# Sums of squares in a two-block transformer kernel: head sums in four column groups, and squares added on GpSimd ahead of two matmuls

## The reference

```
def rms_norm(x, gain):
    y = x * rsqrt(mean(x * x, axis=-1) + EPS)
    return y * gain

# first block
h = h + mixer(rms_norm(h, norm_mix))      # 1st normalisation; w_in, two attentions, w_out
#   inside: fox heads: rms_norm(fq heads, fox_q_gain), rms_norm(fk heads, fox_k_gain)
h = h + peer(rms_norm(h, norm_ffn))       # 2nd; w_query, top-k of keys, peer_u, peer_v
# second block
h = modulate(rms_norm(h, norm1_g), ...)   # 3rd; w_in_2: attention (q, k normalised by head), S5 scan, gates
h = modulate(rms_norm(h, norm2_g), ...)   # 4th; w_up, convolution, w_down
```

## Time and profile before

| | |
|---|---|
| median of 3 runs | 3751.93 us (3750.91 to 3752.04) |
| time of the profiled execution | 3747.92 us |
| its span, first to last instruction | 3746.3 us |
| TensorE matmul busy | 3612.7 us, 96% |
| VectorE busy | 2572.4 us, 69% |
| ScalarE busy | 2113.1 us, 56% |
| GpSimd busy | 71.1 us, 2% |
| mean granted TensorE clock | 0.987 |

### The profile page before, as it was taken

The page is one execution under the profiler, slowest core; times in us unless marked ns, Lnnn a source line. Parts: engine busy times, 40 slices in busy tenths (PEclk is TensorE's granted clock), DMA queues, the critical chain, the costliest instruction groups (busy, mean ns, idle before and its releaser), DMA issues.

```text
span 3746.3 us, 75816 instructions
## 1 busy us (share of the span) xinstructions
PE 3612.7 (96%) x26600; PEld 3390.2 (90%) x26600; DVE 2572.4 (69%) x4815; ACT 2113.1 (56%) x3811; POOL 71.1 (2%) x137
## 2 busy tenths in 40 slices
PE   7999998999999999999999989999988899999998
PEld 6999998999999999787888879889988899999998
DVE  5775647788877777555688868887656666666555
ACT  4446644666667776454555555554554566666453
POOL 1000000000000000000000000000000000000000
PEclk9999999999999999999999999999999999999999
DMA  7854457555554444566788844444444455555554
GB/s 262 313 195 148 149 197 286 187 178 178 176 178 161 159 162 152 173 212 213 269 330 331 328 157 139 154 132 143 148 154 157 148 185 179 182 186 183 175 185 153
DMA packets 183888, 721.09 MB, mean 192 GB/s; under 512 B 20416, under 2 KB 22976, under 8 KB 170688
## 3 DMA queue, kind: packets, MB, share of 16 engines
q1 hardware_dynamic: 166464, 608.57, 48.2%
q0 software_dynamic: 14352, 102.77, 7.6%
q10 hardware_dynamic: 2928, 7.83, 0.6%
HBM read 714.89 MB, written 4.19 MB: 192 GB/s over the span
## 4 chain that ended last, share of the span: by engine, by line
PE 90%; DVE 5%; ACT 2%; issue 1%; DMA 1%; ACTq 0%; DVEq 0%; SPq 0%
PE PS L394 22%; PE PS L396 21%; PE PS L395 21%; PE PS L526 6%; PE PS L527 6%; PE PS L528 6%; PE PS L730 1%; PE PS L779 1%; DVE wlo L1296 1%; ACT whi L900 1%; DVE big L1364 1%; PE PS L539 0%; PE PS L422 0%; PE PS L606 0%; DVE big L1784 0%
## 5 line engine op out<-in xcount | busy, mean ns | idle before, releaser
L900 ACT ACTIVATE whi<-raw 128x512 fp32r<-128x512 f32 x2296 | 1425.0, 629 | 1440.9 <-PE PS L396 1084.8
L1296 DVE TENSOR_TENSOR wlo<-raw,whi 128x512 fp32r<-128x512 f32 x2296 | 1538.3, 690 | 994.5 <-ACT whi L900 981.4
L394 PE MATMUL PS<-hhi,whi 128*128 128x256 f32 (+1 forms) x6976 | 1992.5, 286 | 83.4 <-DVE hlo L1355 21.6
L395 PE MATMUL PS<-hlo,whi 128*128 128x256 f32 (+1 forms) x6976 | 1969.5, 282 | 0.0
L396 PE MATMUL PS<-hhi,wlo 128*128 128x256 f32 (+1 forms) x6976 | 1969.1, 282 | 0.0
L394 PEld LDWEIGHTS PS<-hhi,whi 128*128 128x128 f32 x6976 | 1323.8, 190 | 111.9 <-issue 71.1
L396 PEld LDWEIGHTS PS<-hhi,wlo 128*128 128x128 f32 x6976 | 1324.3, 190 | 0.0
L395 PEld LDWEIGHTS PS<-hlo,whi 128*128 128x128 f32 x6976 | 1320.6, 189 | 0.6
L526 PE MATMUL PS<-whi,hhi 128*128 128x512 f32 x1024 | 404.3, 395 | 4.8 <-issue 3.6
L527 PE MATMUL PS<-wlo,hhi 128*128 128x512 f32 x1024 | 404.3, 395 | 0.0
L528 PE MATMUL PS<-whi,hlo 128*128 128x512 f32 x1024 | 404.1, 395 | 0.0
(11 more groups left out here) (400 smaller groups left out, 2251.2 us busy)
## 6 DMA issues: line engine op xcount, KB each, us to landing
raw<-peer_u_dram SPq DMA_DIRECT2D x256, 512.0 KB, 3.3
raw<-peer_v_dram SPq DMA_DIRECT2D x256, 512.0 KB, 4.3
raw<-w_in_dram SPq DMA_DIRECT2D x240, 512.0 KB, 4.1
big<-w_mod_dram POOLq DMA_DIRECT2D x96, 1024.0 KB, 5.2
raw<-w_up_dram SPq DMA_DIRECT2D x176, 512.0 KB, 3.3
raw<-w_down_dram SPq DMA_DIRECT2D x88, 512.0 KB, 3.3
raw<-w_out_dram SPq DMA_DIRECT2D x64, 512.0 KB, 3.3
raw<-w_query_dram SPq DMA_DIRECT2D x32, 512.0 KB, 4.9
```

Of the source, the lines that this page charges most:

```text
L394: pe.matmul(out, hi, rhi, start=start, stop=False, **more)
L395: pe.matmul(out, hi, rlo, start=False, stop=False, **more)
L900: f(whi[:, m % PAIRS, quarter(q)], raw[:, m % RING, quarter(q)], ACT.Copy).then_inc(hi_ready, 1)
L1296: dv.tensor_tensor(wlo[:, m % PAIRS, quarter(q)], raw[:, m % RING, quarter(q)], whi[:, m % PAIRS, quarter(q)], ALU.subtract).then_inc(lo_r ...
```

## The change

The head sums are written to four groups of 32 PSUM partitions: head 4i + q goes to row 32q + i, with a 128 x 32 stationary window, and neighbouring matmuls go to different groups. Variance, root and spreads then work on 128 partitions. For the second and the fourth normalisation, GpSimd adds squares 1 to 14 to square 0, and TensorE has two matmuls of ones left: the sum tile and the last square. w_out_2 becomes a plain `dense` in a loop, and the L360 transfers from the fifth on stand behind fourteen of the adds on GpSimd's queue.

```
-        onecol = sb("onecol", [P, 31])
+        onecol = sb("onecol", [P, 63])
...
+        added_mid, added_end = sem("added_mid"), sem("added_end")
...
+            def add_tiles(of, squared, added):
+
+                for n in range(1, KC - 1):
+                    pool.wait_ge(squared, n + 1)
+                    pool.wait_ge(added, n - 1)
+                    pool.tensor_tensor(of[:, 0, :], of[:, 0, :], of[:, n, :], ALU.add).then_inc(added, 1)
+
             for kc in range(KC):
+                if kc == MOD_RING:
+                    add_tiles(sq0[:, :, META:], squares_mid, added_mid)
                 pool.wait_ge(modw_used, MOD_EARLY * KC + kc + 1)
                 pool.dma_start(modring_mid[:, kc % MOD_RING, :],
                                d["w_mod"][MOD_EARLY * KC + kc]).then_inc(modw_in[kc % MOD_RING], 16)
...
                 pool.dma_start(bst[:, n % 2, :, :], d["s5_b"][n]).then_inc(bc_in[n % 2], 16)
+            add_tiles(sqb, squares_end, added_end)
...
-            def dense_and_squares(name, chunk0, inputs, of, ready):
-
-                def one_sum(n):
-                    pe.wait_ge(ready, n + 1)
-                    return pe.matmul(PS[:, 7, 0:SEQ], ones[:, :], of[:, n, :], start=n == 0, stop=n == KC - 1)
-
-                for g in range(4):
-                    dense_turn(name, chunk0, SEQ, g, lambda k: one_sum(4 * g + k - 1) if g + k > 0 else None,
-                               inputs if g == 0 else None)
-                one_sum(KC - 1).then_inc(sums, 1)
+            def sum_squares(of, squared, added):
+
+                pe.wait_ge(added, KC - 2)
+                pe.matmul(PS[:, 7, 0:SEQ], ones[:, :], of[:, 0, :], start=True, stop=False)
+                pe.wait_ge(squared, KC)
+                pe.matmul(PS[:, 7, 0:SEQ], ones[:, :], of[:, KC - 1, :], start=False, stop=True).then_inc(sums, 1)
 
             def head_sums(of, width, bank):
 
-                for n in range(16):
-                    o = width - of[n].shape[-1]
-                    last = pe.matmul(PS[0:16, bank, o:width], onecol[:, 15 - n:31 - n], of[n], start=n == 0, stop=n == 15)
+                for i in range(4):
+                    for q in range(4):
+                        o = width - of[4 * i + q].shape[-1]
+                        last = pe.matmul(PS[32 * q:32 * q + 32, bank, o:width], onecol[:, 31 - i:63 - i], of[4 * i + q],
+                                         start=i == 0, stop=i == 3)
                 last.then_inc(head_sum, 1)
 
+            def spread_of(n):
+
+                row = 32 * (n % 4) + n // 4
+                return ident[:, row:row + 1].to_broadcast([P, P])
+
             def head_spread(n, bank, of):
 
                 pe.wait_ge(head_rstd, 1)
-                pe.matmul(PS[:, bank, 0:of.shape[-1]], ident[0:16, n:n + 1].to_broadcast([16, P]), of,
+                pe.matmul(PS[:, bank, 0:of.shape[-1]], spread_of(n), of,
                           start=True, stop=True).then_inc(head_wide, 1)
...
-                    head_spread(8 + h, 6, rstd[0:16, 0, META:KEYS])
-                    head_spread(h, 7, rstd[0:16, 0, 0:KEYS])
+                    head_spread(8 + h, 6, rstd[:, 0, META:KEYS])
+                    head_spread(h, 7, rstd[:, 0, 0:KEYS])
...
-                if n > 0:
-                    square_sum(n - 1)
-            square_sum(KC - 1).then_inc(sums, 1)
+            sum_squares(sq0[:, :, META:], squares_mid, added_mid)
...
-                    last = pe.matmul(PS[:, 7, k * SEQ:(k + 1) * SEQ], ident[0:16, n:n + 1].to_broadcast([16, P]),
-                                     rstd[0:16, 0, 0:SEQ], start=True, stop=True)
+                    last = pe.matmul(PS[:, 7, k * SEQ:(k + 1) * SEQ], spread_of(n),
+                                     rstd[:, 0, 0:SEQ], start=True, stop=True)
...
-            dense_and_squares("w_out_2", 320, None, sqb, squares_end)
+            dense("w_out_2", 320, SEQ)
+            sum_squares(sqb, squares_end, added_end)
...
-                link(dv.tensor_scalar(rstd[0:16, 1, 0:width], PS[0:16, bank, 0:width], 1.0 / P, EPS, ALU.mult, ALU.add))
-                dv.reciprocal(rstd[0:16, 0, 0:width], rstd[0:16, 1, 0:width]).then_inc(head_var, 1)
+                link(dv.tensor_scalar(rstd[:, 1, 0:width], PS[:, bank, 0:width], 1.0 / P, EPS, ALU.mult, ALU.add))
+                dv.reciprocal(rstd[:, 0, 0:width], rstd[:, 1, 0:width]).then_inc(head_var, 1)
```

More of the change, by code:

```diff
@@ L682, in _ @@
                 beside_in(c)
-            def square_sum(n):
-                pe.wait_ge(squares_mid, n + 1)
-                return pe.matmul(PS[:, 7, 0:SEQ], ones[:, :], sq0[:, n, META:], start=n == 0, stop=n == KC - 1)
             pe.wait_ge(modw_used, MOD_EARLY * KC + MOD_RING)
@@ L920, in head_root @@
                 sc.wait_ge(head_var, turn + 1)
-                f(rstd[0:16, 0, 0:width], rstd[0:16, 0, 0:width], ACT.Sqrt).then_inc(head_rstd, 1)
+                f(rstd[:, 0, 0:width], rstd[:, 0, 0:width], ACT.Sqrt).then_inc(head_rstd, 1)
             def split_only(name, tiles):
@@ L1389, in _ @@
             link(dv.memset(onecol[:, :], 0.0))
-            link(dv.memset(onecol[:, 15:16], 1.0))
+            link(dv.memset(onecol[:, 31:32], 1.0))
             link(dv.memset(rstd[:, :, :], 1.0))
```

## The result

| | before | after |
|---|---|---|
| median of the runs, us | 3751.42 (3750.18 to 3752.04, 4 runs) | 3725.65 (3725.07 to 3726.87, 4 runs) |
| profiled execution, us | 3747.92 | 3725.45 |
| its span, us | 3746.3 | 3723.8 |

The ratio is 0.9932 [0.9916, 0.9948]: 25.8 us or 0.7% faster. Predicted were 3723.4 us (3718 to 3734), a gain of 28.5 us. The measurement is 2.2 us above the forecast, inside the range; the gain is 2.7 us short of the forecast.

The account below looks back on a forecast made before the run. TensorE was taken to bound the kernel (busy 96% of the span, 90% of the chain). Gains 6.0 + 5.5 + 10.25 + 3.1 + 2.0 + 1.7 = 28.5 us put the median at 3723.4 us, range 3718 to 3734.

Parts of the forecast that it names:

- Squares of w_out: Second normalisation: 14 square sums of 0.43 us leave TensorE's chain between chunks, 6.0 us gained, nothing in the tail.
- Squares of w_out_2: Fourth normalisation: 14 sums of 0.43 us go, 6.0 us, less 0.5 for the new loop, net 5.5 us.
- The loop step of 0.17 us a turn: w_out_2 as a loop: 0.17 us lost a turn, three turns, 0.5 us, read from the next stage.
- Adds: 28 GpSimd adds of 0.736 us in w_out and w_out_2 cost nothing; without cover they would be 20.7 us.
- Head sums: w_in and w_in_2: four column groups run at once, blocks gain 5.2 and 5.05 us, together 10.25.
- weight loads in turn: Rival on the head sums: loads take turns, a block lasts at least 3.5 us; total gain 25.1 us; chance 0.15.
- groups in turn: Rival on the head sums: column groups take turns wholly, blocks stay 7 us; total gain 18.3 us; chance 0.07.
- Spreads: 128 partitions instead of 16 save about 0.39 us a round: 3.1 us in w_in, 2.0 (0 to 3.1) in w_in_2.
- The rival that spreads gain nothing: Spreads in both input projections gain nothing and the clock stays; total gain 21.7 us, 3730.2; chance 0.07.
- Clock: Half-clock stretches at 193 and 221 us: one of the two goes, 1.7 us, with ends 0 and 3.4.
- Gain handed to other engines: Rival: TensorE's gain in both input projections goes to other engines, only squares' 11.5 us remain, 3740.4; chance 0.06.
- Slower: Rival: fifth w_mod transfer waits for the adds and TensorE starves; 7.5 us loss needs adds of 10.7 us; chance 0.01.

Follow-up runs that it names:

- Experiments 5: The changed kernel with six further GpSimd operations ahead of every add, each multiplying the tile by ones; 3758.5 us.
- Experiment 6: The changed kernel with eight further GpSimd operations ahead of each add, so that the adds fall behind the squares; 3802.33 us.
- Experiment 4: The changed kernel with the two head-sum loops exchanged, all four matmuls of one column group before the next group; 3731.69 us, a single time.
- experiment 3: The kernel before with only the spreads changed, to 128 partitions with zeros on the other rows, no column groups; 3745.44 us, ratio 0.9988.
- experiment 2: The kernel before with only the squares changed (GpSimd adds, two matmuls at both places) and w_out_2 as a loop; 3740.69 us, ratio 0.9973.
- the wider tile: The kernel before with onecol 63 columns wide instead of 31, the wider part never read; peer_u's part takes 392.13 us, no whole time given.
- experiment 9: The changed kernel with VectorE's variance of the second head sums one chunk earlier (chunk 26 instead of 27); 3724.54 us once.

## Why the prediction was right, point by point

**Squares of w_out.** As forecast, 14 times 0.43: 6.0 us. Without the sum, a chunk takes 6.16 us where 6.2 was said.

**Squares of w_out_2.** 5.2 us instead of 5.5, but not for the reason given. The loop step of 0.17 us a turn does not exist there: from its second chunk on, no two dense matmuls of w_out_2 start more than 0.13 us apart in the changed kernel, and the written-out version is as long. The step was read from w_up. It is there in both kernels, but one chunk behind the edge of each turn and not at the edge (with w_up's chunks counted from 0, turns start at 4, 8 and 12, the steps stand at 5, 9 and 13); w_query, a plain loop as well, has none in either. What took 0.5 us is the spacing of the dense matmuls, 0.1183 us on average instead of 0.1176 over some 700 of them. Both the loop and the written-out form have it, so it goes with the sums taken out, not with the loop. It is the spacing of w_query in both kernels, with 5.68 us a chunk, so 6.07 - 5.68 = 0.39 us a sum could have been read before the change. The term of 0.5 us was right in size by luck.

**Adds.** Their price was nothing, and their length 0.742 us against 0.736. Experiments 5 and 6 take the cover away and show what it was: a chunk's time on GpSimd's side, and the free half of VectorE on the other. The bound that an add takes at most its own time from VectorE was sound: seven times the work (70.23 us busy in 84, against 10.13 in 89) added 0.29 us to each of the four splits of a chunk in w_out, where TensorE saw none of it. In w_out_2 the same work made the chunks 0.5 to 0.6 us longer. The 28 real adds cost TensorE nothing in either stage.

**Head sums.** 5.31 and 5.15 against 5.2 and 5.05. The two rivals on them are refuted by the blocks of 1.92 and 1.86 us: weight loads in turn would have needed 3.5, groups in turn 7. The Trainium skill's rule that a load overlaps only with another row group (TensorE: Matmul & The Clock Gate, "Part 3: Packing small matmuls") does not hold for these column groups: 32 loads are hidden in 1.92 us. Experiment 4 adds what I could only assume, that the order round the groups is the condition.

**Spreads.** 3.0 in w_in against 3.1. In w_in_2 1.3 against 2.0, inside the bounds given: the rounds themselves give 1.9 (five of 0.28 and one of 0.47), and chunks between them, each 0.1 to 0.3 us longer, take back 0.6. The rival that spreads gain nothing falls by experiment 3.

**Clock.** I counted one stretch of the two, 1.7 us; both went, about 3.0. Between 186 and 230 us, where the spreads stand, there are one or two such stretches in each of the four executions with spreads on 16 partitions (the kernel before twice, experiment 2, the wider tile), and none in any of the ten with 128. That the narrow spreads bring them is thus well supported; what makes the clock fall is not shown. Later in w_in, from 236 to 326 us, boundaries without spreads do fall in some executions, with either form: in two of the four and in five of the ten. So the prediction's remark that boundaries without spreads show no fall held for the execution it was read from, and not for all.

**What was missing.** Three things. The place of the tiles, -2.36 us, which the diff contained in one number, the width of `onecol`, and which I passed over. Half-clock stretches elsewhere, -5.2 us in the ledger against +1.2 ahead of w_out, where 1.7 either way had been allowed; their number and place differ from execution to execution (236 to 326, 1477 to 1503, 2207 to 2240, 2434 to 2459, 2722 to 2749), with the old blocks as with the new, so none of them is shown to be the change's doing. And the sentence that the saving is the same in the profiled time and in the median failed: 22.5 and 25.8 us, as before's profiled execution lay 3.5 us under its own median and after's only 0.2. These were partly opposite: the sum was 6 us above the ledger, and the median came out 3.3 us better than the ledger. That the forecast lies within 2.2 us of the time is in part luck.

**Range.** Added up, the bounds given (spreads in w_in_2, clock, a shifted fall) make 3718.9 to 3728.8 us, not 3719.5 to 3728; the measured 3725.65 is inside either.

**Gain handed to other engines.** Hardly: the waits of TensorE for VectorE between 2415 and 2500 are 2.9 us in all, and behind the same block before they were 2.5. The low clock that was to speak against the forecast does stand behind the short block in w_in_2 (2436.6), but it is not new with it (experiment 9). **Slower.** Not near: the fifth transfer left 27.15 us after the adds' end, as predicted (28). Experiment 6 shows that late adds first cost at another place than the rival named, TensorE's own wait for the last add. That wait stood in the changed code, and I had not priced it.

**Open.** Why 128 bytes of tile placement cost 2.36 us in a part of peer_u. The operations of ScalarE and VectorE there have the same durations in both, and the dense matmuls are each a little further apart (0.1183 us for 0.1175 over 2714 steps, 2.1 of the 2.36 us). So this part, which had run at a closer spacing, falls to the spacing that w_query has in both kernels. Other shifts than 128 bytes were not tried.

## What to carry to other kernels

Small matmuls packed in column groups should change the group with every instruction: the same 32 records take 1.92 us in that order and 4.74 group after group. A matmul on few partitions amid dense work costs more than its columns (0.37 us a round in w_in), so padding it to 128 partitions with zeros in one operand is a gain even though it computes more. When a diff widens a tile, put the new width where it moves no other tile, and compare the stages that the diff does not touch; reading both traces at equal instructions shows a loss there that medians hide.

## What was not expected of the hardware

- 128 bytes more in front of the tiles lengthen a part of peer_u from 389.77 to 392.13 us with identical instructions; taking them away in the changed kernel brings 389.77 back.
- GpSimd and VectorE slow each other when both are busy: in w_out the split goes from 714 to 1008 ns, GpSimd's add from 742 to 1004 ns; in w_out_2 the split takes 1142 ns, and the chunks grow from 5.68 to 6.2 us.
- Four column groups of fp32 matmuls (128x32) run wholly at once, with 32 records in 1.86 us at 256 columns.
- Spreads on 16 partitions cost 0.37 us a round in w_in, and beside them (186 to 230 us) all four executions had one or two stretches at half clock of 3.4 or 6.8 us; with 128 partitions there was none there in ten.
- Group after group, column groups overlap in twos (4.53 us for 32 records); changing the group with every matmul starts all four within 0.03 us.
